# Two transformer blocks on one core: the order of exponents and chunks in the gated mixer, of latents and last heads in the attention mixer

## What is computed

```python
# gated recurrence, per chunk of 64 tokens: G = cumsum(log forget)
decay = exp(where(causal, G[t] - G[s], -inf))
scores = sum(q[t] * k[s] * decay, axis=-1)
o = (q * exp(G)) @ S + scores @ v
S = exp(G_end) * S + (k * exp(G_end - G)).T @ v
# attention mixer
c_q, c_kv, k_rope, sb_qkv, gates = split(u @ w_in)
q = rms_norm(c_q, g_q) @ w_q_up ; kv = rms_norm(c_kv, g_kv) @ w_kv_up
o_mla = softmax(causal(q @ k.T * scale)) @ v
merged = g_mla * (o_mla @ w_branch_mla) + g_sb * (o_sb @ w_branch_sb)
h = h + merged @ w_out
```

## Time and profile before

| | us |
|---|---|
| median of 3 runs | 2257.95 (2257.26 to 2259.03) |
| the profiled execution | 2261.95 |
| its span | 2260.6 |
| TensorE busy in it | 2215.2 |
| VectorE, ScalarE, GpSimd busy | 828.1, 452.4, 1315.4 |

### The profile page before, as it was taken

How to read it: one execution, slowest core, us unless ns; L and a number is a source line. 1 busy time by engine, 2 the same in 40 slices (tenths; PEclk the granted TensorE clock), 3 DMA queues, 4 the chain that set the end, 5 groups by cost and what they waited for, 6 DMA issues and landing times.

```text
span 2260.6 us, 25908 instructions
## 1 busy us (share of the span) xinstructions
PE 2215.2 (98%) x10938; PEld 1832.6 (81%) x10938; DVE 828.1 (37%) x929; ACT 452.4 (20%) x751; POOL 1315.4 (58%) x772
## 2 busy tenths in 40 slices
PE   8999999989999999999999999999999999999999
PEld 7888888867788888888888888878767888888887
DVE  3334203776443333104443202143566633333013
ACT  3111004323331111003111102013476121111012
POOL 5666664634356666665666665656435656666654
PEclk9999999999999999999999999999999999999999
DMA  5232322212222323232322322222200323323222
GB/s 182 94 102 93 98 98 75 94 48 66 66 84 99 97 93 102 94 96 82 103 94 95 101 93 94 88 90 84 78 1 20 93 84 100 96 94 111 93 86 92
DMA packets 55819, 200.84 MB, mean 89 GB/s; under 512 B 6680, under 2 KB 6808, under 8 KB 55576
## 3 DMA queue, kind: packets, MB, share of 16 engines
q1 hardware_dynamic: 53856, 194.14, 26.7%
q10 hardware_dynamic: 1848, 5.04, 0.6%
HBM read 197.06 MB, written 2.10 MB: 88 GB/s over the span
## 4 chain that ended last, share of the span: by engine, by line
PE 74%; DVE 2%; ACT 1%; issue 1%; POOL 0%; DVEq 0%; ACTq 0%
PE psum L380 15%; PE psum L382 15%; PE psum L381 15%; PE psum L462 7%; PE psum L463 7%; PE psum L461 7%; PE psum L1010 1%; PE psum L960 1%; PE psum L977 1%; PE psum L425 1%; PE psum L1128 1%; PE psum L1130 1%; PE psum L1129 1%; ACT work L1646 0%; PE psum L668 0%
## 5 line engine op out<-in xcount | busy, mean ns | idle before, releaser
L345 POOL TENSOR_TENSOR w_lo<-w_raw,w_hi 128x1024 fp32r<-128x1024 f32 x365 | 884.2, 2422 | 30.4
L343 POOL TENSOR_SCALAR w_hi<-w_raw 128x1024 fp32r<-128x1024 f32 x365 | 387.3, 1061 | 828.1 <-PE psum L382 573.1
L380 PE MATMUL psum<-u_hi,w_hi 128*128 128x512 f32 (+1 forms) x2072 | 792.8, 383 | 1.9 <-DVE u_lo L1747 1.1
L381 PE MATMUL psum<-u_hi,w_lo 128*128 128x512 f32 (+1 forms) x2072 | 787.9, 380 | 0.0
L382 PE MATMUL psum<-u_lo,w_hi 128*128 128x512 f32 (+1 forms) x2072 | 787.7, 380 | 0.0
L380 PEld LDWEIGHTS psum<-u_hi,w_hi 128*128 128x128 f32 x2072 | 391.6, 189 | 79.2 <-issue 4.7
L382 PEld LDWEIGHTS psum<-u_lo,w_hi 128*128 128x128 f32 x2072 | 391.1, 189 | 74.0
L381 PEld LDWEIGHTS psum<-u_hi,w_lo 128*128 128x128 f32 x2072 | 391.3, 189 | 73.7 <-issue 0.8
L461 PE MATMUL psum<-w_hi,hidden_hi 128*128 128x512 f32 x800 | 311.4, 389 | 0.9 <-DVE work L2099 0.9
L462 PE MATMUL psum<-w_lo,hidden_hi 128*128 128x512 f32 x800 | 311.2, 389 | 0.0
L463 PE MATMUL psum<-w_hi,hidden_lo 128*128 128x512 f32 x768 | 298.8, 389 | 0.0
(11 more groups left out here) (287 smaller groups left out, 1549.1 us busy)
## 6 DMA issues: line engine op xcount, KB each, us to landing
w_raw<-in_ffn_in SPq DMA_DIRECT2D x176, 512.0 KB, 3.4
w_raw<-in_ffn_out SPq DMA_DIRECT2D x88, 512.0 KB, 3.4
w_raw<-in_proj_in SPq DMA_DIRECT2D x34, 512.0 KB, 3.4
w_raw<-in_mix_in SPq DMA_DIRECT2D x29, 512.0 KB, 3.3
w_raw<-in_embed SPq DMA_DIRECT2D x10, 512.0 KB, 3.5
w_raw<-in_mix_out SPq DMA_DIRECT2D x8, 512.0 KB, 3.4
w_raw<-in_branch SPq DMA_DIRECT2D x8, 512.0 KB, 3.5
w_raw<-in_proj_out SPq DMA_DIRECT2D x8, 512.0 KB, 3.5
```

The lines of the kernel that those rows point to most:

```text
L343: pool.tensor_scalar(hi, raw, 1.0, 1.0, ALU.mult, ALU.mult).then_inc(k.w_split, 1)
L345: pool.tensor_tensor(lo, raw, hi.bitcast(F32), ALU.subtract).then_inc(k.w_split, 1)
L380: pe.matmul(out, hi[:, cols], xhi, start=first, stop=False)
L381: pe.matmul(out, lo[:, cols], xhi, start=False, stop=False)
```

## The change

On TensorE, the second filling chunk (9) is issued ahead of level 0; the sums of the second latent's squares are issued after projection chunk 12 and not 18; softmax head 7 writes its values to the lower half of bank 5 and not to the upper half of bank 6, and no longer waits for head 6 to be copied out; and a branch chunk takes the tiles in the order 4, 5, 6, 0, 1, 2, 7, 3. On VectorE, exponents(n + 3) stands before multiply(n + 2) for n >= 1; the norm of the second latent and its two scalings come after projection chunks 17 and 18, not 19 and 20; the row maxima of softmax head 0 come before the split of stick-breaking head 0. On ScalarE, the squares, the root and the copies of the second latent all come before the gates of chunks 18 to 20; and the weights of softmax head 7 are divided there and not on GpSimd. Blank lines aside, the whole diff:

```diff
@@ -355,11 +355,13 @@
             pool.tensor_tensor(tile(k.ulo, n), H.o[n], tile(k.uhi, n).bitcast(F32), ALU.subtract).then_inc(k.pair_lo, 1)
     for h in range(AH):
-        pool.wait_ge(k.rs_inv, h + 1)
-        for i, c in ROWS:
-            w = H.probs[:, c:c + (i + 1) * P]
-            d = pool.tensor_scalar(w, w, H.rs[:, h * NT + i:h * NT + i + 1], None, ALU.mult)
-        d.then_inc(k.divided, 1)
+
+        if h < AH - 1:
+            pool.wait_ge(k.rs_inv, h + 1)
+            for i, c in ROWS:
+                w = H.probs[:, c:c + (i + 1) * P]
+                d = pool.tensor_scalar(w, w, H.rs[:, h * NT + i:h * NT + i + 1], None, ALU.mult)
+            d.then_inc(k.divided, 1)
         pairs(h)
@@ -700,8 +702,8 @@
             m.then_inc(k.hd_turned, 1)
     fill(8)
+    fill(9)
     level(0)
-    fill(9)
     pe.wait_ge(k.level_mul, 2)
     turn_heads(g.item(KEYS_ITEM), 0)
     level(1)
@@ -792,7 +794,7 @@
             pe_latent_sums(k, 0, KCQ, 0)
         elif i == 11:
             pe_turn_key_rope(k)
-        elif i == 18:
+        elif i == 12:
             pe_latent_sums(k, KCQ, KCKV, 1)
         elif i == 21:
             pe.wait_ge(k.proj_scaled, 11)
@@ -1030,7 +1032,7 @@
                 pe.wait_ge(k.z_out, h)
         if m is not None:
             pe.wait_ge(k.p_copied, m + 1)
-            if m:
+            if 0 < m < AH - 1:
                 pe.wait_ge(k.o_out, m)
         last = len(CAUSAL_BLOCKS) - 1
         for n, (i, t0, width, c) in enumerate(CAUSAL_BLOCKS):
@@ -1039,7 +1041,7 @@
                 z = pe.matmul(k.ps[7][half(h), t0:t0 + width], v, H.z_at(h, c, width), start=n == 0, stop=n == last, skip_group_check=True)
             if m is not None:
                 v = H.v[:, (m * NT + i) * HV:(m * NT + i + 1) * HV]
-                o = pe.matmul(k.ps[6][half(m), t0:t0 + width], v, H.turned_at(m, c, width), start=n == 0, stop=n == last, skip_group_check=True)
+                o = pe.matmul(softmax_out(k, m)[:, t0:t0 + width], v, H.turned_at(m, c, width), start=n == 0, stop=n == last, skip_group_check=True)
         if h is not None:
             z.then_inc(k.z_values, 1)
         if m is not None:
@@ -1064,6 +1066,11 @@
     values(AH - 1, AH - 1)
+def softmax_out(k, m):
+
+    return k.ps[6][half(m), :] if m < AH - 1 else k.ps[5][half(0), :]
+
+
 def turned_bank(h):
     return B0 if h < AH - 1 else A0
@@ -1079,16 +1086,16 @@
             pe.wait_ge(k.merge_dve, 3 * (j - 2) + 2)
         else:
             pe.wait_ge(k.p_copied, AH)
-        for part in (1, 0):
-            for t in range(4):
-                kk = 4 * part + t
-                if j == 0:
-                    pe.wait_ge(k.pair_hi, KD + PAIRS.index(kk) + 1)
-                    if kk in COMPLETE[AH]:
-                        pe.wait_ge(k.last_lo, COMPLETE[AH].index(kk) + 1)
-                    else:
-                        pe.wait_ge(k.pair_lo, KD + PAIRS.index(kk) + 1)
-                m = mm3(pe, k.ps[b + part], hi, lo, slice(kk * P, (kk + 1) * P), tile(k.uhi, kk), tile(k.ulo, kk), t == 0, t == 3)
+
+        for kk in (4, 5, 6, 0, 1, 2, 7, 3):
+            part, t = kk // 4, kk % 4
+            if j == 0:
+                pe.wait_ge(k.pair_hi, KD + PAIRS.index(kk) + 1)
+                if kk in COMPLETE[AH]:
+                    pe.wait_ge(k.last_lo, COMPLETE[AH].index(kk) + 1)
+                else:
+                    pe.wait_ge(k.pair_lo, KD + PAIRS.index(kk) + 1)
+            m = mm3(pe, k.ps[b + part], hi, lo, slice(kk * P, (kk + 1) * P), tile(k.uhi, kk), tile(k.ulo, kk), t == 0, t == 3)
         m.then_inc(k.w_used, 1)
     def ready(kk):
@@ -1096,7 +1103,7 @@
     def free(i):
         if i == 0:
-            pe.wait_ge(k.p_copied, AH)
+            pe.wait_ge(k.o_out, AH)
         elif i == 1:
             pe.wait_ge(k.z_out, AH)
             pe.wait_ge(k.o_out, AH)
@@ -1517,13 +1524,12 @@
     act_root(k, "ql", k.sc[3][:, :])
     for n in range(KCQ):
         latent_hi(n)
-    gate(18)
     latent_squares(KCQ, KCKV)
-    gate(19)
     act_root(k, "kl", k.sc[3][:, :])
-    latent_hi(KCQ)
-    gate(20)
-    latent_hi(KCQ + 1)
+    for n in range(KCKV):
+        latent_hi(KCQ + n)
+    for i in range(18, 21):
+        gate(i)
     for i in range(21, 34):
         gate(i)
         if i == 21:
@@ -1661,6 +1667,13 @@
                 act.wait_ge(k.z_out, 2 * n - 6)
             act.copy(tile(k.uhi, n), H.o[n]).then_inc(k.pair_hi, 1)
+    def divide(h):
+        act.wait_ge(k.rs_inv, h + 1)
+        for i, c in ROWS:
+            w = H.probs[:, c:c + (i + 1) * P]
+            a = act.activation(w, w, ACT.Copy, scale=H.rs[:, h * NT + i:h * NT + i + 1])
+        a.then_inc(k.divided, 1)
+
     act.preload_act_table_set("natural_log_exp_and_others")
     exponents(0)
     for h in range(1, AH):
@@ -1668,6 +1681,8 @@
         weigh(h - 1)
         exponents(h)
         act_soft_hi(k, h)
+        if h == AH - 1:
+            divide(h)
         pairs(h)
     weigh(AH - 1)
     pairs(AH)
@@ -1954,11 +1969,14 @@
     dve.wait_ge(k.qf_taken, 8)
     dve.tensor_tensor(g.item(1), q, kk, ALU.mult).then_inc(k.level_mul, 1)
     multiply(KEYS_ITEM)
-    for n in range(last + 1):
+    multiply(2)
+    keep(0)
+    exponents(3)
+    for n in range(1, last + 1):
+        if n + 3 < QUERIES_ITEM:
+            exponents(n + 3)
         multiply(n + 2)
         keep(n)
-        if n + 3 < QUERIES_ITEM:
-            exponents(n + 3)
         if n >= 4:
             remember(2 * (n - 4))
             remember(2 * (n - 4) + 1)
@@ -2194,10 +2212,10 @@
             dve_key_rope(k)
         elif i == 15:
             dve_masks(k)
-        elif i == 19:
+        elif i == 17:
             latent_norm("kl", KCQ, KCKV, 1)
             latent(3, "kv_latent", 0)
-        elif i == 20:
+        elif i == 18:
             latent(4, "kv_latent", 1)
         elif i == 25:
             dve_softplus(k, 0)
@@ -2329,7 +2347,7 @@
     def mla_out(h):
         dve.wait_ge(k.o_values, h + 1)
-        dve.tensor_copy(H.o[h // 2][half(h), :], k.ps[6][half(h), :]).then_inc(k.o_out, 1)
+        dve.tensor_copy(H.o[h // 2][half(h), :], softmax_out(k, h)).then_inc(k.o_out, 1)
     def split(h):
         dve.wait_ge(k.soft_hi, h + 1)
@@ -2345,8 +2363,8 @@
             dve.wait_ge(k.pair_hi, KD + PAIRS.index(n) + 1)
             dve.tensor_tensor(tile(k.ulo, n), H.o[n], tile(k.uhi, n).bitcast(F32), ALU.subtract).then_inc(k.last_lo, 1)
+    maxima(0)
     split(0)
-    maxima(0)
     divide(0)
     for h in range(1, AH):
         add_sums(h - 1)
```

## The result

The changed kernel takes 2239.07 us (median of four runs, 2238.28 to 2243.82) against 2257.61 us (2257.18 to 2259.03) for the kernel before beside it. The ratio is 0.9921, 95% interval 0.9904 to 0.9938: faster by 17.8 us, give or take 4. The forecast was 2237.8 us in a range of 2233.0 to 2245.0. The profiled execution took 2243.82 us with a span of 2242.5, against 2261.95 and 2260.6 before: 18.1 us less.

The account below looks back on a forecast made before the run. TensorE, with work in 98% of the span, bounds the kernel; only its waits and overlong work can be saved. Savings of 12.6 + 3.6 + 0 + 4.0 = 20.2 us off the 2257.95 median give 2237.8 us, range 2233.0 to 2245.0.

Parts of the forecast that it names:

- A: Gated mixer levels: exponents ahead and chunk 9 before level 0 remove waits and half clock; 12.6 us, bounds 9 to 13.3.
- B: Second latent: earlier squares, sums and norm remove TensorE's 2.0 us wait and the half clock behind; 3.6 us, 1 to 3.7.
- D: Last softmax heads: division on ScalarE 1.1, values side by side 2.0, no wait for head 6 0.9; 4.0 us.
- the 5.4 us one: TensorE's wait ahead of the state products at L632, levels 4 and 5, claimed to vanish; 5.4 us.
- The half clock of 3.1 us: Time lost to low clock after the long wait at the state products, claimed to go with it; 3.1 us.
- rival 4: Mixer levels: VectorE and GpSimd lock each other out, splits come late, filling chunks wait; 2262 to 2268 us, chance 0.03.
- The quiet price: Mixer levels: VectorE's second subtraction pair ahead of multiply(3) was counted as unblocked by GpSimd, 1.2 us per subtraction.
- C: First softmax head: row maxima before the split gain nothing, as exponents wait for ScalarE's table load; 0 us.
- rival 2: Half-clock stretches move to another sparse piece instead of vanishing; 3.1 + 1.7 us given back, 2242.6 us, chance 0.08.
- 1: Mixer levels: exponents ahead are themselves late, TensorE waits at each of five levels; 2243 us, chance 0.14.
- 3: Last two heads don't overlap, or the branch's tile 7 is late; 2.0 to 2.5 us lost, 2240.2 us, chance 0.08.
- 5: More than the sum: other low-clock stretches, near 558 and 1653, fall elsewhere as well; 2233 us, chance 0.07.

Follow-up runs that it names:

- third chunk: The whole change plus one more filling chunk ahead of level 2, so later levels stand one chunk later; 2246.05 us, ratio 0.9950 to the kernel before.
- the levels alone: The kernel before with only the exponents ahead and chunk 9 in front of level 0; 2250.69 us, ratio 0.9967.

## Why the prediction was right, step by step

**The total** came within 1.3 us of the median, and that is in part luck. By the distances A is worth 6.6 to 8 us for 12.6 forecast, B 2.2 or 3.9 for 3.6, D 4.7 for 4.0: 13.5 to 16.6 us for 20.2. The rest of the measured gain is clock, and not all of that is the change's own.

**A, levels: the mechanism right, the size of one wait wrong.** The chain, the exponential's 2.0 us hidden, the new wait at level 2 and kv(6) within 0.7 us all came as worked out. The step that failed is "the 5.4 us one" in "waits 1.3 + 3.4 + 5.4 = 10.1": it was read from a single execution. In three other profiles with unedited levels the wait was 2.2 us (two) or none (one), and kv(6) began at 502.9 to 504.2, so in them the edits of A bring 6.6 to 8 us, not 12.6. Level 0 itself starts up to 0.8 us apart in these profiles (434.69 to 435.46); measured from there the exponents are worth 5.4 to 6.6 us, and the chunk 0.9. The half clock of 3.1 us, the other term read from the single execution, belonged to the wait of 5.4 us; in the three others it lay on level 3, where it was partly covered. VectorE's idle ahead of L1909, which was to vanish, did so at levels 2 and 3; at levels 4 and 5 it is 1.46 and 2.75 us, at no cost, since TensorE is the later one there. The new wait was 1.1 us for 0.6: the held first subtraction 2.13 us, 0.9 of it beyond its own 1.2, was foreseen; but the four subtractions and two multiplications start behind VectorE's masked copy, at 444.17, and not at the end of the turned keys, at 443.4, from which I had counted.

Of the lock rule (the Trainium skill, "SBUF — State Buffer", section "SBUF: two separate sides") the rows show more than I used. In the list above L345 took 6.82 us from 461.07: VectorE's rows beside it are these:

```profile
461.01 1.21 DVE L1913 TENSOR_TENSOR work<-work 128x1024 f32<-128x1024 f32 x1
...
464.41 1.22 DVE L1925 TENSOR_TENSOR work<-work 128x1024 f32<-128x1024 f32 x1
465.55 1.35 DVE L1935 COPY_PREDICATED scratch_f<-const,psum 128x1024 f32<-128x1024 uint32 x1
466.80 2.18 DVE L1913 TENSOR_TENSOR work<-work 128x1024 f32<-128x1024 f32 x1
```

VectorE's subtraction began 0.06 us ahead of L345, and four two-input instructions ran at their bare 1.2 us until 465.5; L345 ended at 467.89, its free 2.38 us after that; and VectorE's next subtraction, from 466.80, ended 1.1 us behind it, 2.18 us long. The masked copy between them, which reads PSUM, took its usual 1.35 us while L345 ran. By the rule of the Trainium skill whoever starts first has the port for the whole instruction and the other fully blocks. The trace agrees, and shows besides that GpSimd did not get in between VectorE's instructions either. It cost nothing here, since no wait for GpSimd follows on TensorE. This was rival 4's mechanism, and it is no accident of one execution: in all seven kernels with the exponents ahead and no third chunk this L345 took 6.80 to 6.83 us, and in none with unedited levels more than 3.3 us there. It met my sign for a wrong forecast, "if L345 grows beyond 3.5 us in the mixer", and the sign was badly chosen: a longer split costs only if TensorE waits for it, and the kernel before already had one of 4.30 us, at 435.62.

The prediction also says that "a subtraction is held only while GpSimd's L345 runs". That reading is too narrow. The profile of before has GpSimd's other instruction, L343, beside a multiplication of level 3:

```profile
460.65 1.80 POOL L343 TENSOR_SCALAR w_hi<-w_raw 128x1024 fp32r<-128x1024 f32 x1 [4.53 <-PE psum L382]
461.46 2.06 DVE L1910 TENSOR_TENSOR work<-work 128x1024 f32<-128x1024 f32 x1
```

L343 is 1.05 us and L1910 1.22 us where they are alone; here both are about 0.8 us longer. The quiet price for the second pair of subtractions came true all the same.

**B, latents: right, and its two halves separated.** The wait brings 149.96 - 147.76 = 2.2 us for 1.9 forecast. The half clock at the sums, 1.7 us, is there in three of six profiles with unedited latents (151.55 to 151.67), so on average it is half the term that I took in full: B is 2.2 us, or 3.9, and the profile pair had the second.

**C: right**, 0.

**D, last heads: right, 4.7 us for 4.0.** Side by side, together with the wait for head 6's copy, is 3.2 us for 2.9, the division 1.46 for 1.1, the order a cover of 1.6 us, which the sum had rightly left out. The division was undersized because I took only the idle time in brackets, and the transposes came 1.42 us sooner.

**The clock.** A run's time lost to it can be estimated from its granted clock, as time x (1 - clock), with about 1 us of rounding: 11.5 us on average over 47 runs of the kernel before, 6.7 us over the four runs of the changed kernel. A single reading can be wrong: one run of the levels alone has 0.946 at 2250.69 us, with its neighbours at 0.995 and 0.996 and the same time; it is left out below. The Trainium skill ("TensorE: Matmul & The Clock Gate", section "Terms") gives that kind of product as the penalty, the time at a reduced clock by what is missing of it; in direction the trace agrees, level 3's 64 products taking 2.09 us at full clock and up to 3.68 where part of them ran at half. Taken off, the kernels stand at 2246.3 and 2233.3 us on average: by this estimate **13.0 us of the gain are waits and overlap** (by the distances 2.2 + 4.7, which leaves 6.1 for the levels, where the kernel with the levels alone gives 7.0), and 4.8 are clock. The forecast had 15.4 us of waits and overlap and 4.8 of clock. But the clock's share isn't safe, with four runs of the changed kernel: by the same estimate the kernel that differs in nothing but C loses 11.2 us to the clock, and the one without the new order 7.8. The 4.8 agree with the forecast in size and not in place: low stretches did vanish from the state products and the latents, and others appeared near 581 and 1612 us. That is rival 2 in part, and the 18.1 of the profile pair against 20.4 of its three distances (11.95, 3.8, 4.7) is its price, 2.3 us.

**Rivals.** 1 fell: L610 waits once for VectorE, not at several levels. 2 is true in part. 3 fell: the 28 products last 2.4 us and no wait stands ahead of the branch's chunks. 4 did not come about in time, though L345 was stretched as it says. 5 did not come about: the gain is below the sum.

What stays open: why a stretch of low clock falls on level 3 in one execution and behind the state products in another, and whether it decides the length of the wait there. No run settled it.

## What to carry to other kernels

When two engines alternate in a chain, put the step whose result a third engine needs longest ahead of the step that waits, and count the waits of the level in which the chain is behind. Before a wait is added to a sum, look at it in a second profile of the same kernel: here one was 5.4 us in one profile and absent in the next. For edits of one to three microseconds in a program of over two thousand, measure the distance between two instructions on either side of the edit, and compare it where the clock in between is the same: at the latents and the last heads it repeated to 0.1 us, where total times of one kernel scatter by 13.

## What the runs showed of the hardware that was not expected

- GpSimd's weight subtraction, 2.38 us alone, took 6.82 us beside four of VectorE's two-input instructions without a gap, and 6.80 to 6.83 in the other six kernels with the exponents ahead and no third chunk.
- The same program's stretches of half clock lie elsewhere from execution to execution, and runs of one kernel at a mean granted clock of 0.996 and of 0.994 are 8 us apart (medians of 2254.4 and 2262.1 us for the kernel before).
- An execution with an early low stretch can be ahead later on: kv(6) began at 508.22 where level 3's scores ran at full clock, and at 502.85 to 504.23 where they ran partly at half. Four profiles show the pairing, none its cause.
